# Rotary turn of queries and keys by small SBUF transfers in place of a matmul

## The reference

```python
def partial_rope(x, cos, sin):
    half = ROT_DIM // 2            # ROT_DIM = 16 of the 64 rows of a head
    x1, x2, rest = x[..., :half], x[..., half:ROT_DIM], x[..., ROT_DIM:]
    return jnp.concatenate([x1 * cos - x2 * sin, x2 * cos + x1 * sin, rest], -1)

proj = u @ w_in                    # q, k, v, glu_in, g_attn, g_conv
q = partial_rope(q...); k = partial_rope(k...)
attn = moba_attention(q, k, v)     # 256 positions: one causal block
y_conv = conformer_conv(glu_in, ...)   # depthwise, 31 taps, 512 channels
merged = sigmoid(g_attn) * (attn @ w_attn_br) + sigmoid(g_conv) * y_conv
```

## Time and profile before

| quantity | value |
|---|---|
| median of three runs | 1775.1 us |
| the profiled execution | 1772.67 us |
| its span, first to last instruction | 1770.9 us |
| granted TensorE clock, mean | 0.995 |
| TensorE busy | 1739.6 us, 98% |
| VectorE busy | 1369.8 us, 77% |
| ScalarE busy | 923.0 us, 52% |
| GpSimd busy | 288.9 us, 16% |

### The profile page before, as it was taken

The page is one execution under the profiler, slowest core; times in us unless marked ns, Lnnn a source line. Parts: engine busy times, 40 slices in busy tenths (PEclk is TensorE's granted clock), DMA queues, the critical chain, the costliest instruction groups (busy, mean ns, idle before and its releaser), DMA issues.

```text
span 1770.9 us, 26770 instructions
## 1 busy us (share of the span) xinstructions
PE 1739.6 (98%) x11266; PEld 1556.7 (88%) x11266; DVE 1369.8 (77%) x1842; ACT 923.0 (52%) x1149; POOL 288.9 (16%) x219
## 2 busy tenths in 40 slices
PE   8999999999999999999999999999999999999998
PEld 7888898988888888889888898898888998998887
DVE  6997644798789887687988779878755699778754
ACT  6554465655455544566554444756543536556432
POOL 1000000220210001050000139600000089100000
PEclk9999999999999999999999999999999999999999
DMA  8667433466676667525666644344555443445552
GB/s 285 258 260 260 171 143 120 176 257 262 239 275 263 260 233 264 190 96 185 243 262 234 242 163 142 125 170 149 189 186 187 149 165 140 143 143 190 182 186 84
DMA packets 53815, 348.41 MB, mean 197 GB/s; under 512 B 6833, under 2 KB 10434, under 8 KB 13762
## 3 DMA queue, kind: packets, MB, share of 16 engines
q1 hardware_dynamic: 53122, 345.68, 53.3%
q10 hardware_dynamic: 576, 1.05, 0.2%
HBM read 345.65 MB, written 1.05 MB: 196 GB/s over the span
## 4 chain that ended last, share of the span: by engine, by line
PE 87%; DVE 8%; ACT 3%; DMA 1%; POOL 1%; issue 0%; SPq 0%; ACTq 0%; DVEq 0%; POOLq 0%
PE bank L928 40%; PE bank L927 21%; PE bank L883 7%; PE bank L885 7%; PE bank L884 7%; DVE wl L1963 2%; DVE bank L2450 1%; ACT wh L1495 1%; DVE arena L2469 1%; DMA raw<-in_chunks 1%; PE bank L1438 1%; DMA x<-in_x 0%; DVE arena L2468 0%; DVE arena L2497 0%; PE bank L1263 0%
## 5 line engine op out<-in xcount | busy, mean ns | idle before, releaser
L1963 DVE TENSOR_TENSOR wl<-raw,wh 128x2048 fp32r<-128x2048 f32 (+1 forms) x278 | 638.4, 2298 | 249.3 <-ACT wh L1495 248.7
L928 PE MATMUL bank<-xx,wh 128*128 128x512 f32 x1920 | 670.7, 393 | 0.0
L1495 ACT ACTIVATE wh<-raw 128x2048 fp32r<-128x2048 f32 (+1 forms) x278 | 524.1, 1886 | 229.8 <-DMA raw<-in_chunks 229.7
L927 PE MATMUL bank<-xx,wl 128*128 128x256 f32 x1920 | 540.2, 281 | 4.0 <-DVE wl L1999 2.4
L928 PEld LDWEIGHTS bank<-xx,wh 128*128 128x128 f32 x1920 | 359.7, 187 | 81.4
L928 PE MATMUL bank<-hx,wh 128*128 128x512 f32 x1216 | 426.1, 393 | 0.0
L927 PEld LDWEIGHTS bank<-xx,wl 128*128 128x128 f32 x1920 | 362.7, 189 | 7.1 <-DVE xx L1986 2.8
L927 PE MATMUL bank<-hx,wl 128*128 128x256 f32 x1216 | 339.8, 279 | 0.1
L883 PE MATMUL bank<-xx,wh 128*128 128x256 f32 x1008 | 293.3, 291 | 2.9 <-DVE xx L2391 1.5
L885 PE MATMUL bank<-xx,wl 128*128 128x256 f32 x1008 | 287.1, 285 | 0.0
L884 PE MATMUL bank<-xx,wh 128*128 128x256 f32 x1008 | 287.0, 285 | 0.0
(11 more groups left out here) (336 smaller groups left out, 1939.2 us busy)
## 6 DMA issues: line engine op xcount, KB each, us to landing
raw<-in_chunks SPq DMA_DIRECT2D x262, 1024.0 KB, 4.8
arena<-in_ada SPq DMA_DIRECT2D x48, 1024.0 KB, 6.9
raw<-in_chunks SPq DMA_DIRECT2D x16, 768.0 KB, 4.2
arena<-in_bias_rows SPq DMA_DIRECT2D x1, 2048.0 KB, 13.8
raw<-in_chunks ACTq DMA_DIRECT2D x4, 256.0 KB, 7.9
x<-in_x SPq DMA_DIRECT2D x4, 256.0 KB, 8.5
arena<-in_w_uk SPq DMA_DIRECT2D x1, 1024.0 KB, 4.8
arena<-in_w_uv SPq DMA_DIRECT2D x1, 1024.0 KB, 8.9
```

The lines of the kernel that those rows point to most:

```text
L927: pe.matmul(o[:, 0:T], lo_w, halves[:, 0, :], start=start, stop=False, skip_group_check=True)
L928: return pe.matmul(o.rearrange("p (h t) -> p h t", h=2), hi_w, halves, start=False, stop=stop, skip_group_check=True)
L1495: act.activation(wh[:, c % RING, at], raw[:, c % RING, at], ACT.Copy).then_inc(hi_made.sem, 1)
L1963: dve.tensor_tensor(wl[:, c % RING, at], raw[:, c % RING, at], wh[:, c % RING, at].bitcast(F32), ALU.subtract).then_inc(lo_made.sem, 1)
```

## The change

The products with `turn` go, and with them the constant itself. ScalarE issues four transfers for the queries and four for the keys, each of 8 partitions by two slots, which put row i + 8 of each head where row i is and the reverse, in the slots `pm[:, 10:14]` (those of gate chunks 10 to 13, free until then). The missing sign is carried by the sine: the frequencies of the first eight rows are negative. GpSimd clears these four slots at the start of the stage. VectorE waits for the transfers and takes the turned rows from `pm` where it took them from PSUM. ScalarE waits for the clearing, before the keys' transfers also for the queries' sums, and before chunk 10 for all four sums.

```diff
-            turn[first + half + i, first + i] = -1.0
-            turn[first + i, first + half + i] = 1.0
+            freq[first + half + i] = np.float32(500000.0 ** (-2 * i / ROT))
+            freq[first + i] = -freq[first + half + i]
...
+    X_TURNED = X_GA - X_Q
...
-                                 (freq, A["rope_freq"]), (turn, A["rope_turn"])):
+                                 (freq, A["rope_freq"])):
...
         def pool_mix(s):
+            pool.wait_ge(proj_out.sem, proj_out.at(s, 1))
+            pool.memset(pm[:, X_Q + X_TURNED:X_Q + X_TURNED + 4, :], 0.0).then_inc(rope_cleared.sem, 1)
...
         def pe_mix(s, moving):
-            def turned(first):
-                for i in range(2):
-                    n = first + i
-                    pe.wait_ge(proj_out.sem, proj_out.at(s, n + 1))
-                    if first == X_K:
-                        pe.wait_ge(rope_dve.sem, rope_dve.at(s, i + 1))
-                    for m in range(2):
-                        last = pe.matmul(bank[6 + i][:, m * T:(m + 1) * T], turn, pm[:, n, m * T:(m + 1) * T], start=True, stop=True)
-                    last.then_inc(rope_pe.sem, 1)
...
         def act_mix(s):
+            def turned(first):
+                act.wait_ge(proj_out.sem, proj_out.at(s, first + 2))
+                act.wait_ge(rope_cleared.sem, rope_cleared.at(s))
+                if first == X_K:
+                    act.wait_ge(rope_dve.sem, rope_dve.at(s, 2))
+                for head in (0, HD):
+                    for row in (0, ROT // 2):
+                        to, of = head + row, head + ROT // 2 - row
+                        act.dma_start(pm[to:to + ROT // 2, first + X_TURNED:first + X_TURNED + 2, :],
+                                      pm[of:of + ROT // 2, first:first + 2, :]).then_inc(rope_moved.sem, 16)
...
+                elif step in ("ropeq", "ropek"):
+                    turned(X_Q if step == "ropeq" else X_K)
+            act.wait_ge(rope_dve.sem, rope_dve.at(s))
...
         def rope(first):
-                    dve.wait_ge(rope_pe.sem, rope_pe.at(s, (first - X_Q) + i + 1))
+                    dve.wait_ge(rope_moved.sem, rope_moved.at(s, 4 * 16 * (1 + (first - X_Q) // 2)))
-                    dve.tensor_tensor(t, split(bank[6 + i][:, :]), two(sinT), ALU.mult)
+                    dve.tensor_tensor(t, split(pm[:, n + X_TURNED, :]), two(sinT), ALU.mult)
```

More of the change, by code:

```diff
@@ L73, in constants @@
     freq = np.zeros((P, 1), np.float32)
-    turn = np.zeros((P, P), np.float32)
     for first in range(0, P, HD):
         for i in range(half):
-            freq[first + i] = freq[first + half + i] = np.float32(500000.0 ** (-2 * i / ROT))
-            turn[first + half + i, first + i] = -1.0
-            turn[first + i, first + half + i] = 1.0
-    return bucket, {"rope_freq": freq, "rope_turn": turn}
+            freq[first + half + i] = np.float32(500000.0 ** (-2 * i / ROT))
+            freq[first + i] = -freq[first + half + i]
+    return bucket, {"rope_freq": freq}
 def tiles(w):
@@ L251, in build @@
     part_turns, posi = posi, posi.bitcast(I32)
-    turn, freq = even_const[:, 6 * T:6 * T + P], even_const[:, 6 * T + P:6 * T + P + 1]
+    freq = even_const[:, 6 * T:6 * T + 1]
     c = Carver(FF2_TILES * 2 * T)
@@ L417, in build @@
     conv_made = signal("conv_made")
-    rope_pe = signal("rope_pe")
+    rope_moved = signal("rope_moved")
+    rope_cleared = signal("rope_cleared")
     rope_dve = signal("rope_dve")
@@ L468, in build @@
             conv_made.plan(s, CONV_K * 2 + (CONV_K - POOL_TAPS) * 2)
-            for g, n in ((rope_pe, 4), (rope_dve, 4), (ao_made, 4), (cln_pe, 2), (cln_act, 2 + CT), (cln_dve, 1 + CT),
+            for g, n in ((rope_cleared, 1), (rope_moved, 2 * 4 * 16), (rope_dve, 4), (ao_made, 4), (cln_pe, 2), (cln_act, 2 + CT), (cln_dve, 1 + CT),
                          (xh_made, 2 + 2 + 4), (xl_made, 2 + 2 + 4), (merged, 4), (tile_done, 1), (x_ready, KT)):
@@ L804, in pool_rope @@
         def pool_rope():
-            pool.wait_ge(rope_loaded.sem, 16 * 3)
+            pool.wait_ge(rope_loaded.sem, 16 * 2)
             link(pool.tensor_copy(turns, posi))
@@ L1344, in pe_mix @@
             c0 = base[s]
-            def turned(first):
-                for i in range(2):
-                    n = first + i
-                    pe.wait_ge(proj_out.sem, proj_out.at(s, n + 1))
-                    if first == X_K:
-                        pe.wait_ge(rope_dve.sem, rope_dve.at(s, i + 1))
-                    for m in range(2):
-                        last = pe.matmul(bank[6 + i][:, m * T:(m + 1) * T], turn, pm[:, n, m * T:(m + 1) * T], start=True, stop=True)
-                    last.then_inc(rope_pe.sem, 1)
-            todo = {"ropeq": lambda: turned(X_Q), "ropek": lambda: turned(X_K)}
             for step in MIX:
@@ L1362, in pe_mix @@
                     pe_chunk(s, step, c0 + step, step in (8, 9))
-                elif step in todo:
-                    todo[step]()
             pe.wait_ge(proj_out.sem, proj_out.at(s, 10))
```

## The result

The changed kernel takes 1778.77 us (median of 20 runs, 1775.29 to 1782.51) against 1774.55 us for the kernel before in runs beside it. The ratio is 1.0027, interval 1.0020 to 1.0034: 4.8 us slower, 3.5 to 6.0. The forecast was 1789 us, 14 above before: the sign was right, the size three times too large, and 0.27% lies just inside what I had called the same. The profiled execution of after took 1780.52 us, its span 1778.7.

The account below looks back on a forecast made before the run. VectorE's unbroken run from chunk 8 to the normalisation, not TensorE, was taken to bound the mixer stages. 1772.67 + 2 x (7.5 + 0.3) = 1788.3 us, stated as 1789; own range 1783 to 1796, wide range 1778 to 1799.

Parts of the forecast that it names:

- the same: Whole kernel: changes within 0.3% (5.3 us) can't be told from none; this outcome was given 0.10.
- What bounds the kernel, and what the removal is worth: Mixer stages: VectorE sets the time, so removing TensorE's turn, 7.2 us at the most, gains nothing.
- The operation that decides: First rotary product on VectorE: reading two SBUF tiles, it must take turns with GpSimd's instructions; +7.5 us per stage.
- the walk: VectorE and GpSimd alternating, operation by operation, from the queries' rotary operations to the normalisation: 1101.9 in place of 1094.4.
- L832 until 1059.34; L2467 1059.88: Start of the queries' rotary operations: GpSimd's instruction finishes first, VectorE's first product waits and ends at 1059.88.
- holds `lo` 10 until about 1074.45: After chunk 9's taps: GpSimd holds VectorE's `lo` 10, which before started at once; about 1.1 us.
- keys' turn: Keys' rotary operations on VectorE: a hold of 0.9 us, then alternation with GpSimd, ending 1088.4; before, 1081.00.
- queries' turn, over 6.3 us: Queries' rotary operations on VectorE: alternation with GpSimd ends them at 1067.9 in place of 1064.75, +3.15 us.
- phase allowance: Whether `lo` 10 and the keys' first operation meet a GpSimd instruction: about 1.1 us each, 5.5 to 9 per stage.
- The transfers are late: Queries' turn: transfers landing 4.8 us or more after issue add 2 to 4 us per stage, 1792 to 1797; 15%.
- What TensorE does meanwhile, and the clock: Mixer stage: the 3.6 us saved go into TensorE's waits, over 10 us; half clock taken as zero, up to 3 us.
- Nothing is given back: After the transposes: TensorE's shift stays; VectorE's 4.0 us wait for GpSimd's taps goes, without helping TensorE.

Follow-up runs that it names:

- run 1: Kernel before with TensorE's turn (32 matmul instructions) left out, turned rows not computed: 1773.49 us, ratio 0.9999.
- run 2: Changed kernel with the sine copied once per stage into PSUM, so the first rotary product reads one PSUM operand: 1775.02 us, ratio 1.0013.
- runs 5, 6: GpSimd's taps 2 to 27 left out, of the kernel before (1763.9 us, ratio 0.9931) and of the changed kernel (1759.35 us, ratio 0.9916).
- second profile: Changed kernel run again unchanged, to profile it once more: 1778.98 us, ratio 1.0033.
- run 9: Changed kernel with VectorE's taps of steps 4 to 7 split 5, 7, 5, 7 in place of 6 each: 1785.97 us, ratio 1.0069.
- run 3: Changed kernel with sine, cosine and the product of the turned rows in PSUM: 1769.38 us, ratio 0.9981.
- 7: Kernel before, turn still on TensorE, with cosine and the product of the turned rows in PSUM: 1770.94 us, ratio 0.9984.
- run 8: Changed kernel with sine, cosine and product in PSUM and 25 taps on GpSimd in place of 27: 1764.21 us, ratio 0.9938.
- 11: Kernel before, turn still on TensorE, with cosine and product in PSUM and 25 taps on GpSimd: 1772.51 us, ratio 0.9987.

## Why the prediction was right or wrong

**What bounds the kernel, and what the removal is worth.** Right: nothing (run 1), because VectorE's run lies through both turns.

**The operation that decides.** Right in kind. The product with two SBUF tiles takes turns with GpSimd: with its operand back in PSUM the run of VectorE is the old one (run 2), and with GpSimd silent it costs no more than from PSUM (runs 5, 6). What the Trainium skill says in "SBUF — State Buffer", section "SBUF: two separate sides", holds in these runs in that one side waits for the whole instruction of the other. That whoever starts first gets the pair, as the same section has it, does not hold by the starts that the profile shows: GpSimd was 0.03 to 0.06 us ahead in the eight turns of the two profiles of after and lost seven.

**The step that failed is the start of each hold in the walk**, in the sentence "L832 until 1059.34; L2467 1059.88" and in "holds `lo` 10 until about 1074.45". I took it that an instruction of GpSimd that began 0.1 us earlier had the right of way, and I called the phase of `lo` 10 and of the keys' turn uncertain. That neither holds could have been read in the trace of before. At `lo` 10, which VectorE started at 1070.08, GpSimd's timeline of before has

```profile
1070.03 3.48 POOL L834 TENSOR_TENSOR arena<-arena 128x512 f32<-128x512 f32 x1
```

an L834 that had begun ahead of it, and still `lo` 10 ran in 2.19 us and L834 was held. GpSimd is released at the end of each `lo`. It then ends the instruction that was held and runs one more, about 2.2 us together (`lo` 8 ends at 1056.07, the second L832 begins at 1058.30), and VectorE's six taps take 2.36: both engines come to the next clash within 0.1 us of each other, each time. In that dead heat VectorE won seven turns of eight in the two profiles of after, and `lo` 10 every time. The terms were:

| term, per stage | predicted | mix0 | mix1 | second profile |
|---|---|---|---|---|
| queries' turn, over 6.3 us | +3.15 | +1.2 | +3.1 | +1.2, +1.2 |
| hold of `lo` 10 | +1.1 | 0 | 0 | 0, 0 |
| keys' turn | +3.2 | +1.2 | +1.2 | +1.2, +1.2 |
| run of VectorE | +7.5 | +2.3 | +4.3 | +2.4, +2.4 |

Four cheap turns make 4 x 1.2 = 4.8 us, which is what the ratio gives (4.8). With GpSimd 0.4 us ahead in the heat the kernel is 12.2 us slower (run 9): the walk was right for a case that the kernel mostly does not meet. My phase allowance (5.5 to 9 per stage) held neither stage, because I varied only where the holds fall and never let VectorE win the first one. That 1778.77 us still lies in the wide range of 1778 to 1799, by 0.8 us, is luck: its lower end was drawn to leave out no more than two in ten, and no term of the walk reaches it. The narrower range doesn't add up either. From 1789 the phases and 3 us of clock give 1785 to 1795, where I wrote 1783 to 1796, and the clock's "up to 3 us per stage" is counted there once.

**The transfers and ScalarE.** "The transfers are late" did not happen: landing took 3.1 us at most, and issue ran beside `hi`; the 0.3 us per stage were nothing. ScalarE's waits cost nothing that shows: run 2 keeps them all, and its mix0 is as long as before.

**What TensorE does meanwhile, and the clock.** The waits of mix0 came where they were named: 0.5 us for `lo` 9 (2.5 predicted), 1.6 for the keys' sums (5), 2.4 for `lo` 11 (2), 1.7 for the transposes, 6.3 in all where I had named over 10. From chunk 5's evacuation to the transposes it is 45.4 us, before 43.1, where I had named 50. The clock did fall, in this stretch of after (columns as in the earlier trace rows),

```profile
1086.00:1088.00 2.00, 2.00 (x11) 2.00 (x11) 2.00 (x4) 0.00 (x0) 2.00 (x1) 0.50 0.00 0
```

to 1.2 GHz while chunk 11 was multiplied, after TensorE had stood for the scores and for `lo` 11. Chunk 11 was done by 1092.68, ahead of the transposes at 1094.66, so it cost nothing, as taken.

**Nothing is given back.** Right for after (the stages' loss is that of the run), though VectorE's wait of 4.0 us for GpSimd's taps, which I said would go, stayed at 4.0. Run 3 shows the other side of it: of 5 us won on VectorE per stage 3 to 4 are given back to GpSimd, which I had named as ending late and not as the next limit.

## What to carry to other kernels

When an operand moves from PSUM to SBUF, look at what GpSimd does in that stretch before anything else: the price here is whole GpSimd instructions, and it vanished wherever one of the two inputs was in PSUM. If two engines meet periodically, compare the two periods; where they agree to 0.1 us the clash is a dead heat each time, so price both outcomes and read in the old trace who has been winning. A saving on an engine that is busy for 98% is worth something only where that engine ends last. Here it brought nothing while VectorE was late (run 1), next to nothing once GpSimd became late in its place (run 3 against 7), and its price or a little more when both were out of the way (run 8 against 11). Two kernels of the same time can have different limits; the chain that ended last tells them apart.

## What the runs showed of the hardware

- A GpSimd instruction that began 0.03 to 0.06 us before a VectorE operation on two SBUF tiles lost to it in seven turns of eight, and then to the one issued directly behind it as well (2.22 us for an L834 of 1.04); once, 0.04 us ahead, it won. Begun 0.43 us before, it won four of four. Where the border lies wasn't measured.
- The same VectorE product on 128x512 takes 0.67 to 0.69 us with one input in PSUM beside a busy GpSimd, 0.68 to 0.69 with both in SBUF and GpSimd's taps left out, and 0.68 to 1.78 us with both in SBUF beside GpSimd (runs 2, 6 and after).
- ScalarE's queue issues transfers while a ScalarE activation issued ahead of them is still running: 0.14 us after the start of one of 1.91 us.
